# A weight prologue with its own buffers, half loads and row-wise waits, and a row-max chain one step later on VectorE

## Time and profile before

| | |
|---|---|
| Median of three runs | 1796.87 us |
| The profiled execution's own time | 1797.72 us |
| Its span, first to last instruction | 1795.9 us |
| Mean granted TensorE clock | 0.961 of full speed |
| TensorE (matmul) busy | 1614.9 us, 90% |
| VectorE busy | 1180.6 us, 66% |
| ScalarE busy | 1132.3 us, 63% |
| GpSimd busy | 542.1 us, 30% |
| DMA | 154.71 MB, mean 86 GB/s |

### The profile page before, as it was taken

How to read it: one execution, slowest core, us unless ns; L and a number is a source line. 1 busy time by engine, 2 the same in 40 slices (tenths; PEclk the granted TensorE clock), 3 DMA queues, 4 the chain that set the end, 5 groups by cost and what they waited for, 6 DMA issues and landing times. The chain is left out here.

```text
span 1795.9 us, 38276 instructions
## 1 busy us (share of the span) xinstructions
PE 1614.9 (90%) x14224; PEld 946.3 (53%) x14224; DVE 1180.6 (66%) x1458; ACT 1132.3 (63%) x1458; POOL 542.1 (30%) x282
## 2 busy tenths in 40 slices
PE   4599999999997299999999999999999999959998
PEld 2265555555554046555655565556555655634444
DVE  4554544545545578888888888888888888632332
ACT  5454455445544178877888787878787887852332
POOL 0000000000000055555556565556555655610000
PEclk8799999999999589999999999999999999979999
DMA  6212212312202933223322332233232332236553
GB/s 221 100 59 66 74 57 65 93 38 84 79 22 71 187 113 75 59 58 86 73 58 62 81 73 59 70 73 73 62 73 66 75 70 62 50 103 187 180 166 122
DMA packets 244894, 154.71 MB, mean 86 GB/s; under 512 B 63728, under 2 KB 228080, under 8 KB 244848
## 3 DMA queue, kind: packets, MB, share of 16 engines
q1 hardware_dynamic: 244848, 154.10, 32.2%
HBM read 111.95 MB, written 41.97 MB: 86 GB/s over the span
## 5 line engine op out<-in xcount | busy, mean ns | idle before, releaser
L863 POOL TENSOR_TENSOR p_pl<-p_p,p_ph 128x1024 f16<-128x1024 f32 x192 | 482.3, 2512 | 1027.5 <-ACT p_ph L900 947.7
L915 DVE TENSOR_REDUCE p_part<-p_mx 128x2 f32<-128x1024 f32 x384 | 468.2, 1219 | 139.2 <-PE p_mx L991 86.5
L891 ACT ACTIVATE p_p<-p_st 128x1024 f32<-128x1024 f32 x384 | 391.9, 1021 | 175.8 <-PE p_st L1022 79.6
L515 PE MATMUL p_ring<-p_w_hi,p_xT 128*128 128x512 f16 (+3 forms) x1536 | 392.7, 342 | 34.7 <-issue 19.1
L900 ACT ACTIVATE p_ph<-p_p 128x1024 f16<-128x1024 f32 x336 | 355.2, 1057 | 21.6
L945 DVE TENSOR_TENSOR p_pl<-p_p,p_ph 128x1024 f16<-128x1024 f32 x192 | 274.5, 1430 | 10.2 <-ACT p_ph L900 10.2
L515 PE MATMUL p_ring<-p_w_lo,p_xT 128*128 128x512 f16 (+3 forms) x768 | 262.6, 342 | 0.0
L515 PEld LDWEIGHTS p_ring<-p_w_hi,p_xT 128*128 128x128 f16 x1536 | 152.3, 99 | 154.4 <-issue 42.6
L1054 PE MATMUL p_acc<-p_vas,p_ph 128*128 128x129 f16 x2048 | 210.3, 222 | 0.0
L1054 PEld LDWEIGHTS p_acc<-p_vas,p_ph 128*128 128x128 f16 x2048 | 182.5, 98 | 42.5 <-issue 24.2
L1055 PE MATMUL p_acc<-p_vas,p_pl 128*128 128x65 f16 x2048 | 203.5, 194 | 0.0
(11 more groups left out here) (135 smaller groups left out, 2309.4 us busy)
## 6 DMA issues: line engine op xcount, KB each, us to landing
p_vbs<-scratch_vb SPq DMA_DIRECT2D x16, 1028.0 KB, 6.3
p_xin<-in_x SPq DMA_DIRECT2D x16, 512.0 KB, 3.7
scratch_g<-p_g SPq DMA_DIRECT2D x16, 512.0 KB, 3.1
p_kb<-scratch_kb SPq DMA_DIRECT2D x32, 256.0 KB, 5.2
p_gt<-scratch_g SPq DMA_DIRECT2D x16, 512.0 KB, 4.9
p_xr<-in_x SPq DMA_DIRECT2D x16, 512.0 KB, 4.2
out<-p_res SPq DMA_DIRECT2D x16, 512.0 KB, 3.0
p_w_raw<-in_w_in SPq DMA_DIRECT2D x3, 2048.0 KB, 8.4
```

Of the source, the lines that this page charges most:

```text
L515: last = pe.matmul(ring[n % 3][:, 0:w], a, b, start=(m == 0), stop=(m == len(terms) - 1))
L863: pool.tensor_tensor(pl[:, s % NP, :, :].rearrange("p a b -> p (a b)"), p32[:, s % N32, :], ph[:, s % NP, :, :].rearrange("p a b -> p (a b ...
L891: act.activation(p32[:, s % N32, :], st[:, s % 2, :, :].rearrange("p a b -> p (a b)"), ACT.Exp, scale=scale).then_inc(s_exp, 1)
L915: dve.tensor_reduce(part[:, 2 * c:2 * c + 2], mx[:, :, :], AX, ALU.max).then_inc(s_red, 1)
```

## The change

Phase 1:

- The pieces are prepared in another order: cq, ckv, uq, ukv, aq, akv, ag, bg. The raw data of uq and ukv go into two parts of `zT`, a tile that is not written before the second tile of tokens. The six pieces of w_in take turns in the two raw buffers.
- Each load is two DMAs, one for each half of the row blocks, with a semaphore of its own. A reload of a buffer still waits until both engines are through with its last piece. ScalarE starts a half when that half has landed.
- ScalarE and VectorE count row blocks instead of pieces. VectorE starts a row block when ScalarE has done that one, and TensorE starts the three matmuls of a row block when its low part is there.
- Five pieces are split ahead of the first tile. akv is then split where akv was, ag where ag was, and bg at the end. The loads of the rotary table and of the head gains stand after ag's load.

Phase 2: `reduce` no longer runs `max_done`. That stands in VectorE's order one step later, after the reduction of the next pair and ahead of `hi` and `lo`: in steps 5, 13 and 21. `part` gets three slots, since the next unit's first pair is now reduced before the chain.

```diff
-        s_w = [sem("w_loaded0"), sem("w_loaded1")]
+        s_w = [[sem(f"w{r}_half{b}_loaded") for b in range(2)] for r in range(4)]
...
+        WORDER = ["cq", "ckv", "uq", "ukv", "aq", "akv", "ag", "bg"]
...
+                slot = sum(1 for r in slots if r < 2) % 2
+                raw = w_raw[:, slot, 0:KT * w]
...
+                slot, raw = 2, zT[:, 0:9, :].rearrange("p a b -> p (a b)").bitcast(F32)
...
+                slot, raw = 3, zT[:, 9:21, :].rearrange("p a b -> p (a b)").bitcast(F32)
...
+        def half(n, b):
+
+            m = (depth[n] + 1) // 2
+            return slice(0, m) if b == 0 else slice(m, depth[n])
...
-                if n >= 2:
-
-                    sp.wait_ge(s_whi, n - 1)
-                    sp.wait_ge(s_wlo, n - 1)
-                sp.dma_start(raw, src).then_inc(s_w[n % 2], 16)
+                if turns[n] > 0:
+
+                    before = max(m for m in range(n) if slots[m] == slots[n])
+                    sp.wait_ge(s_whi, rows_before[before + 1])
+                    sp.wait_ge(s_wlo, rows_before[before + 1])
+                for b in range(2):
+                    sp.dma_start(raw[:, half(n, b), :], src[:, half(n, b), :]).then_inc(s_w[slots[n]][b], 16)
                 if n == 1:
                     sp.dma_start(xin[:, 1, :], xt[1]).then_inc(s_x[1], 16)
+                if n == 6:
                     sp.dma_start(trg[:, 0, :], trt[0]).then_inc(s_trig[0], 16)
                     sp.dma_start(gains[:, :], g_heads.partition_broadcast(P)).then_inc(s_gains, 16)
...
-                act.wait_ge(s_w[n % 2], n // 2 * 16 + 16)
-                for k in range(raw.shape[1]):
-                    op = act.activation(hi[:, k, :], raw[:, k, :], ACT.Copy, scale=gain[:, k:k + 1])
-                op.then_inc(s_whi, 1)
+                for b in range(2):
+                    act.wait_ge(s_w[slots[n]][b], turns[n] * 16 + 16)
+                    for k in range(depth[n])[half(n, b)]:
+                        act.activation(hi[:, k, :], raw[:, k, :], ACT.Copy, scale=gain[:, k:k + 1]).then_inc(s_whi, 1)
...
-                dve.wait_ge(s_whi, n + 1)
-                for k in range(raw.shape[1]):
-                    op = dve.scalar_tensor_tensor(out=lo[:, k, :], in0=raw[:, k, :], scalar=gain[:, k:k + 1],
-                                                  in1=hi[:, k, :], op0=ALU.mult, op1=ALU.subtract)
-                op.then_inc(s_wlo, 1)
+                for k in range(depth[n]):
+                    dve.wait_ge(s_whi, rows_before[n] + k + 1)
+                    dve.scalar_tensor_tensor(out=lo[:, k, :], in0=raw[:, k, :], scalar=gain[:, k:k + 1],
+                                             in1=hi[:, k, :], op0=ALU.mult, op1=ALU.subtract).then_inc(s_wlo, 1)
...
+            def weights(piece, k):
+
+                pe.wait_ge(s_whi, rows_before[WORDER.index(piece)] + k + 1)
+                pe.wait_ge(s_wlo, rows_before[WORDER.index(piece)] + k + 1)
...
+                for k, terms in enumerate(steps):
+                    if new:
+                        weights(piece, k)
...
-        part = sb("part", [P, 2 * MPAIRS])
+        part = sb("part", [P, 3, 2 * MPAIRS])
...
-                dve.tensor_reduce(part[:, 2 * c:2 * c + 2], mx[:, :, :], AX, ALU.max).then_inc(s_red, 1)
-                if c == MPAIRS - 1:
-                    max_done(i, e // MPAIRS, start)
+                dve.tensor_reduce(part[:, e // MPAIRS % 3, 2 * c:2 * c + 2], mx[:, :, :], AX, ALU.max).then_inc(s_red, 1)
...
-                        reduce(i, s + LEAD, first and s + LEAD < HALF)
+                        reduce(i, s + LEAD)
+                    if (s + LEAD) % MPAIRS == 0 and not (last and s + LEAD > HALF):
+                        max_done(i, (s + LEAD) // MPAIRS - 1, first and s + LEAD <= HALF)
                     if s in DVE_HI:
                         hi(i, s, first)
```

More of the change, by code:

```diff
@@ L160, in phase1 @@
         w3 = w_in.rearrange("l (k p) n -> (l p) k n", p=P)
-        pieces = []
-        for name in PORDER[0:5] + ["uq", "ukv"] + PORDER[5:]:
-            raw = w_raw[:, len(pieces) % 2, :]
+        WORDER = ["cq", "ckv", "uq", "ukv", "aq", "akv", "ag", "bg"]
+        pieces, slots, turns = [], [], []
+        for name in WORDER:
             if name in PROJ:
                 c0, w = PROJ[name]
-                pieces.append((raw[:, 0:KT * w].rearrange("p (k n) -> p k n", k=KT), w3[:, :, c0:c0 + w], gin,
+                slot = sum(1 for r in slots if r < 2) % 2
+                raw = w_raw[:, slot, 0:KT * w]
+                pieces.append((raw.rearrange("p (k n) -> p k n", k=KT), w3[:, :, c0:c0 + w], gin,
                                w_hi[:, :, c0:c0 + w], w_lo[:, :, c0:c0 + w]))
             elif name == "uq":
-                pieces.append((raw[:, 0:3 * 384].rearrange("p (k n) -> p k n", k=3),
+                slot, raw = 2, zT[:, 0:9, :].rearrange("p a b -> p (a b)").bitcast(F32)
+                pieces.append((raw.rearrange("p (k n) -> p k n", k=3),
                                w_uq.rearrange("l (k p) n -> (l p) k n", p=P), gcq, uq_hi, uq_lo))
             else:
-                pieces.append((raw[:, 0:2 * 768].rearrange("p (k n) -> p k n", k=2),
+                slot, raw = 3, zT[:, 9:21, :].rearrange("p a b -> p (a b)").bitcast(F32)
+                pieces.append((raw.rearrange("p (k n) -> p k n", k=2),
                                w_ukv.rearrange("l (k p) n -> (l p) k n", p=P), gckv, ukv_hi, ukv_lo))
-        PIECE = {"cq": 1, "ckv": 2, "aq": 3, "akv": 4, "ag": 5, "uq": 6, "ukv": 7, "bg": 8}
+            turns.append(slots.count(slot))
+            slots.append(slot)
+        depth = [piece[0].shape[1] for piece in pieces]
+        rows_before = [sum(depth[:n]) for n in range(len(pieces) + 1)]
+        def half(n, b):
+            m = (depth[n] + 1) // 2
+            return slice(0, m) if b == 0 else slice(m, depth[n])
         def loop(eng, body):
@@ L326, in tile @@
                 if new:
-                    split_hi(4)
+                    split_hi(6)
                 if not (first and h == 0):
@@ L368, in _ @@
             x_hi(0, 0)
-            for n in range(3):
+            for n in range(5):
                 split_hi(n)
@@ L435, in tile @@
                 if first and h == 0:
-                    for n in range(4, 8):
+                    for n in range(6, 8):
                         split_lo(n)
@@ L509, in _, with project @@
         def _(pe):
-            def project(t, n, w, terms, new):
+            def weights(piece, k):
+                pe.wait_ge(s_whi, rows_before[WORDER.index(piece)] + k + 1)
+                pe.wait_ge(s_wlo, rows_before[WORDER.index(piece)] + k + 1)
+            def project(t, n, w, piece, steps, new):
                 if not (new and n < 3):
                     pe.wait_ge(s_ring, t * 9 + n - 2)
-                for m, (a, b) in enumerate(terms):
-                    last = pe.matmul(ring[n % 3][:, 0:w], a, b, start=(m == 0), stop=(m == len(terms) - 1))
+                for k, terms in enumerate(steps):
+                    if new:
+                        weights(piece, k)
+                    for m, (a, b) in enumerate(terms):
+                        last = pe.matmul(ring[n % 3][:, 0:w], a, b, start=(k == 0 and m == 0),
+                                         stop=(k == len(steps) - 1 and m == len(terms) - 1))
                 last.then_inc(s_proj, 1)
@@ L519, in proj_in @@
                 c0, w = PROJ[name]
-                if new:
-                    pe.wait_ge(s_whi, PIECE[name])
-                    pe.wait_ge(s_wlo, PIECE[name])
                 cols = slice(c0, c0 + w)
[L524 to L528, removed]
+                steps = [[(xT[:, h, 0, k, :], w_hi[:, k, cols]), (xT[:, h, 0, k, :], w_lo[:, k, cols]),
+                          (xT[:, h, 1, k, :], w_hi[:, k, cols])] for k in range(KT)]
+                project(t, n, w, name, steps, new)
             def transpose_x(t, h):
@@ L587, in tile @@
                 pe.wait_ge(s_lt, t + 1)
[L588 to L594, removed]
+                steps = [[(latT[:, k, :], uq_hi[:, k, :]), (latT[:, k, :], uq_lo[:, k, :]), (latT[:, 3 + k, :], uq_hi[:, k, :])]
+                         for k in range(3)]
+                project(t, 5, 384, "uq", steps, new)
                 for n in range(2):
                     cols = slice(384 * n, 384 * n + 384)
[L597 to L601, removed]
+                    steps = [[(latT[:, 6 + k, :], ukv_hi[:, k, cols]), (latT[:, 6 + k, :], ukv_lo[:, k, cols]),
+                              (latT[:, 8 + k, :], ukv_hi[:, k, cols])] for k in range(2)]
+                    project(t, 6 + n, 384, "ukv", steps, new)
                 if not new:
@@ L922, in max_done @@
                 dve.wait_ge(s_red, (u + 1) * MPAIRS)
-                dve.tensor_reduce(rowmax[:, :], part[:, :].rearrange("p (j k) -> p j k", k=4), AX, ALU.max).then_inc(s_md, 1)
```

(5 more changed lines are left out.)

12 lines of the change are left out of this document (5 added, 7 removed).

## The result

The kernel after takes 1826.47 us (median of four runs, 1825.45 to 1829.48), against 1796.13 for the kernel before in the same comparison: ratio 1.0174, 95% interval 1.0157 to 1.0192. The forecast was 1786, its range ended at 1800. The span of the profiled execution is 1823.7 us (1795.9 before).

A forecast was written before the change was run, and what follows sets the result against it. TensorE is busy for 90% of the span, so time can only be won where it stands still or runs at the lower clock. -26 + 10.4 + 0 + 4 = -11.6 us against 1797.7 gives 1786 us; range 1762 to 1800.

The forecast's parts named there:

- Phase 1, 26 us gained: Weight preparation before phase 2: bg's projection starts near 51 us instead of 81.10; 26 us gained, bounds 20 and 29.
- The rival that held the prologue to be hidden: Phase 1: engine order holds bg back, only 13 us are won and phase 2 takes them; 1798 us; chance 0.12.
- Steps 4 to 5: Phase 2, chain moved into step 5: TensorE waits 0.65 us more in sixteen iterations, +10.4 us.
- Steps 12 to 13: Phase 2, chain moved to step 13: step 14's wait goes, step 15's grows to 2.4 us; sum 0, bounds -9 and +5.
- Steps 20 to 21: Phase 2, chain moved to step 21, where GpSimd is idle; VectorE's low part starts just ahead of GpSimd's; 0 us.
- The clock: Phase 2: one 2.4 us idle stretch lowers the clock in three more iterations; +4 us, from 0 to 13.
- GpSimd gets in ahead: Step 21: GpSimd's low part precedes VectorE's, TensorE loses 1.9 us in each of 16 iterations; 1816 us; chance 0.11.
- The chain's move pays: Phase 2: step 14's wait goes, step 5's is covered; up to 0.6 us gained in 15 iterations; 1762 to 1771; chance 0.2.

The follow-up runs named there:

- f1: e1 with each weight piece loaded in one transfer instead of two halves; 1770.1 us.
- f2: e1 with VectorE and TensorE waiting for whole weight pieces instead of row by row; 1790.6 us.
- f3: e1 with uq and ukv put back into the two shared raw buffers, in the new order; 1775.0 us.
- e4: The kernel after with only the chain in step 5 late; those of steps 12 and 20 stand at their old places; 1821.8 us.
- e1: The new phase 1 of the kernel after with the phase 2 of the kernel before; 1768.1 us.
- e7: The kernel after plus one wait: GpSimd begins its low part of step 7 only when VectorE has finished that of step 6; 1784.6 us.
- e3: The kernel after with the chain of step 5 back in step 4; those of steps 13 and 21 stay late; 1771.8 us.
- g1: e1 plus one wait: GpSimd begins its low part of step 13 only when VectorE has finished that of step 12; 1736.3 us.

## Why the prediction was wrong, point by point

- **Phase 1, 26 us gained: right.** The first exponential comes 26.6 us earlier. VectorE's aq was forecast to end at 29.7 and ended at 29.4, bg's split at 56.2 and ended at 56.0; bg was to start near 51 on TensorE (51.54), the second tile's latents at 75.5 (75.42). The rival that held the prologue to be hidden falls. The eight more DMA issues cost nothing, as the sum had it: without them (f1) the kernel is no faster. The weights were partly wrong, though: the text put the buffer that ukv waits for first, and in f2 and f3 taking out the waits by row costs three times as much as taking out the buffers.
- **Steps 4 to 5, +10.4 us: the step that failed.** "TensorE waits 0.65 us more" is right for step 7: 0.86 or 0.87 instead of 0.27, some 9.6 us in 16 iterations. Wrong was to stop there, at an upper bound of 0.65 x 16 + 1. I followed the 0.65 us to TensorE and not on to the next pair of low parts, where 0.32 us of VectorE's lead over GpSimd decided who goes first. VectorE's low part of step 6 then takes 3.17 us instead of 1.22, and waits of 1.62 and 0.63 us in steps 9 and 11 add 36 us. The step's cost is 46 us of idleness; e4, with this step alone, is 54 over e1, and e7, which takes only the queueing away, gives 42 back.
- **Steps 12 to 13, 0: right.** The wait in step 14 is gone, that in step 15 is 2.25 us (2.4 forecast), and the rows arrive 0.22 us late in some iterations ("nearly none" of the cover left). 2.25 + 0.22 - 0.60 - 1.68 = 0.19 us, 3 us in all at most; with steps 20 to 21, e3 measures 3.7. One row was misread without effect: the 0.27 us of step 7 belong to group B's pairs and not to the 35.1 us of the earlier trace rows; those hold 0.34 us of step 13 instead.
- **Steps 20 to 21, 0: right**, by e3. In the kernel after, VectorE's low part there still begins ahead of GpSimd's (1037.64 and 1037.96).
- **The clock, +4 us: near where only the delay is left, too small for the kernel after.** Take the 14 iterations from step 7 of the second to step 7 of the last. In e1, 5 of them ran at a granted clock of 0.97 and TensorE was busy for 788.7 us; in e7 it was 9 and 793.8 us, in after 8 (one of them at 0.95) and 797.9 us. So this term is about 5 of the 15.4 us between the spans of e1 and e7, and about 9 of the 56.6 between e1 and after. The waits make the rest, by the sum of one iteration at most 48.6 us (0.60 + 1.62 + 0.63 + 0.19, times 16).
- **The rivals.** "GpSimd gets in ahead" had the mechanism, the price for one operation and the sign, at 0.11, but I looked for it only in step 21, where the chain itself passes GpSimd's operation. It happened in step 6, where the chain had already done its work and only its delay arrived. "The chain's move pays" falls: the named wait moved one pair on, at the same sum.
- With the queueing taken out (e7) the time is 1784.6, next to the 1786 forecast: 9.5 us under before where 11.6 were forecast. What was missing was one interaction and not a duration.

## What to carry to other kernels

When work is moved on an engine that shares an interface with another, follow the delay until it has died out: past the first wait that it lengthens, to every place within the loop where both engines start a conflicting operation, and write down who leads by how much. A lead of 0.3 us here was worth 42 us. Where the order matters and the other engine has slack, fix it with a semaphore: one such wait, placed at the 3.06 us low part of the kernel before, brought more (32 us) than the whole prologue. And in a prologue whose pieces feed each other in a chain, as here, a whole-piece wait costs its lag again at each link (4.8, 9.6, 15.0 and 25.1 us in f2), so price the fine waits along the whole chain, and not at its end alone.

## What the runs showed of the hardware

- Two operations that read two SBUF tensors, one on VectorE and one on GpSimd, do not slow each other down in these traces, they take turns, whole operations at a time, first come first served. VectorE's low part takes 1.22 us alone, and 1.09 plus what is left of GpSimd's 2.13 when GpSimd began first (3.17, 3.06, 2.17); GpSimd's takes more than 2.13 when VectorE is ahead (2.89). By the Trainium skill, SBUF — State Buffer, "Who interferes with whom", the port pair that the two share is an exclusive lock; these rows agree, and show it held for the whole operation.
- A small operation waits as long as a large one. In step 13 of the kernel after, four elements per partition take 2.05 us behind GpSimd, where they take 0.16 alone (step 5, at 993.28). Timelines of VectorE, then GpSimd:

```profile
1014.48 0.51 DVE L935 TENSOR_SCALAR p_mpair<-p_rowmax 128x4 f16<-128x4 f32 x1
1015.03 2.05 DVE L937 SCALAR_TENSOR_TENSOR p_mpair<-p_rowmax,p_mpair 128x4 f16<-128x4 f32 x1
1017.00 1.21 DVE L953 TENSOR_TENSOR p_pl<-p_p,p_ph 128x1024 f16<-128x1024 f32 x1
```

```profile
1014.36 0.61 POOL L865 TENSOR_TENSOR p_yout<-p_ysum,p_rden 128x256 f32<-128x256 f32 x1 [0.25 <-POOL p_ysum L857]
1014.93 2.13 POOL L873 TENSOR_TENSOR p_pl<-p_p,p_ph 128x1024 f16<-128x1024 f32 x1
```

- Operations of VectorE that read only one SBUF tensor can wait too. The first of VectorE's rows above takes 0.51 us, until GpSimd's output operation ends, and 0.17 alone (at 993.08). In the kernel before, VectorE's high part (L937) takes 0.68 us in steps 5 and 11, and 1.49 in step 18 (at 1032.78), behind a GpSimd operation that runs from 1031.43 to 1033.72.

- The reductions of the pairs, which read PSUM, stayed at 1.19 to 1.23 us in every order.
- Taking waits away paid more than the waits: from e1 to g1 they are 1.68 us shorter in 14 iterations (1.52 in the first of these), 23 us in all, and the time fell by 32. The five iterations of 60.1 us that e1 still had, at a granted clock of 0.97, are gone.
